# Decode attention over paged latents: pages laid over 32 partitions, values split around the next scores, one maximum per row, and all page loads issued by SP

## The reference

```python
def mla_paged_attn(q_nope, q_rope, ckv, krope, w_uk, w_uv, cache_ckv, cache_krope, page_table):
    past_ckv = cache_ckv[page_table].reshape(B, -1, KV_LORA)      # 8 samples x 4096 tokens x 256
    past_kr = cache_krope[page_table].reshape(B, -1, QK_ROPE)     # ... x 32
    q_lat = jnp.einsum('blhd,chd->blhc', q_nope, w_uk)
    s_past = (jnp.einsum('blhc,btc->bhlt', q_lat, past_ckv)
              + jnp.einsum('blhr,btr->bhlt', q_rope, past_kr)).astype(jnp.float32) * ATTN_SCALE
    s_new = (...) # the same against the sample's own new token
    p = jax.nn.softmax(jnp.concatenate([s_past, s_new], axis=-1), axis=-1)
    o_lat = (jnp.einsum('bhlt,btc->blhc', p[..., :T], past_ckv)
             + jnp.einsum('bhls,bsc->blhc', p[..., T:], ckv))
    return jnp.einsum('blhc,chd->blhd', o_lat, w_uv)
```

## Time and profile before

| | us |
|---|---|
| median of 3 runs (1593.17 to 1598.28) | 1594.5 |
| the profiled execution, its own time | 1593.95 |
| its span in the trace | 1592.3 |
| PE busy | 1354.5 (85%) |
| DVE busy | 979.7 (62%) |
| ACT busy | 638.1 (40%) |
| POOL busy | 220.3 (14%) |

### The profile page before, as it was taken

How to read it: one execution, slowest core, us unless ns; L and a number is a source line. 1 busy time by engine, 2 the same in 40 slices (tenths; PEclk the granted TensorE clock), 3 DMA queues, 4 the chain that set the end, 5 groups by cost and what they waited for, 6 DMA issues and landing times. The chain is left out here.

```text
span 1592.3 us, 26749 instructions
## 1 busy us (share of the span) xinstructions
PE 1354.5 (85%) x9613; PEld 1084.7 (68%) x9613; DVE 979.7 (62%) x1338; ACT 638.1 (40%) x856; POOL 220.3 (14%) x322
## 2 busy tenths in 40 slices
PE   5989999786688877766789982899999999937997
PEld 4989999776344444333568872687888888825886
DVE  5456556663577765454244445788888888845653
ACT  5222434320366611101232100777777777743221
POOL 6000221051100032232000000000000000012210
PEclk9999999898799988878779995899999999977999
DMA  5121111375994055464262221479656999935410
GB/s 185 31 79 41 57 67 54 126 251 155 283 371 113 1 169 161 143 217 152 80 226 106 96 90 66 148 263 363 230 211 235 331 404 405 379 143 214 159 67 40
DMA packets 121049, 275.20 MB, mean 173 GB/s; under 512 B 23601, under 2 KB 44594, under 8 KB 120626
## 3 DMA queue, kind: packets, MB, share of 16 engines
q1 hardware_dynamic: 100578, 200.64, 37.1%
q0 software_dynamic: 17200, 61.63, 10.9%
q10 hardware_dynamic: 3168, 11.54, 1.8%
HBM read 214.34 MB, written 58.38 MB: 171 GB/s over the span
## 5 line engine op out<-in xcount | busy, mean ns | idle before, releaser
L399 PE MATMUL pb<-xH,wH 128*128 128x344 f32 x432 | 143.1, 331 | 25.1 <-DVE wL L858 11.0
L401 PE MATMUL pb<-xH,wL 128*128 128x344 f32 x432 | 140.8, 326 | 0.0
L400 PE MATMUL pb<-xL,wH 128*128 128x344 f32 x432 | 140.8, 326 | 0.0
L1621 DVE STREAM_TRANSPOSE pgT<-pages 128x2304 f32<-128x2304 f32 x32 | 81.8, 2570 | 83.4 <-DMA pages<-in_cache 74.5
L2463 DVE TENSOR_TENSOR downL<-raw_down,downH 128x2048 fp32r<-128x2048 f32 x44 | 98.9, 2288 | 45.2 <-ACT downH L2365 45.2
L1492 PE MATMUL pb<-pgT,q 32*8 32x256 f32 x2304 | 79.1, 432 | 44.6 <-DVE pgT L1621 41.9
L2365 ACT CAST gateH<-raw_gate 128x2048 fp32r<-128x2048 f32 x44 | 83.9, 1911 | 67.5 <-PE pb L2298 41.5
L2463 DVE TENSOR_TENSOR gateL<-raw_gate,gateH 128x2048 fp32r<-128x2048 f32 x44 | 100.5, 2287 | 15.8 <-ACT gateH L2365 15.8
L399 PEld LDWEIGHTS pb<-xH,wH 128*128 128x128 f32 x432 | 83.8, 194 | 27.3 <-issue 10.9
L2463 DVE TENSOR_TENSOR upL<-raw_up,upH 128x2048 fp32r<-128x2048 f32 x44 | 100.3, 2281 | 1.0 <-ACT upH L2365 1.0
L1492 PEld LDWEIGHTS pb<-pgT,q 32*8 32x8 f32 x2304 | 41.5, 94 | 81.8 <-DVE pgT L1621 44.9
(11 more groups left out here) (436 smaller groups left out, 3246.7 us busy)
## 6 DMA issues: line engine op xcount, KB each, us to landing
raw_gate<-in_w_gate SPq DMA_DIRECT2D x32, 1024.0 KB, 7.4
raw_up<-in_w_up SPq DMA_DIRECT2D x32, 1024.0 KB, 7.8
raw_down<-in_w_down SPq DMA_DIRECT2D x32, 1024.0 KB, 8.0
pages<-in_cache SPq DMA_DIRECT2D x144, 144.0 KB, 3.6
y_d<-yzero POOLq DMA_DIRECT2D x4, 4096.0 KB, 31.7
pages<-in_cache POOLq DMA_DIRECT2D x112, 144.0 KB, 3.7
y_d<-yo ACTq DMA_DIRECT2D x22, 512.0 KB, 4.1
wraw_p<-in_w_blk SPq DMA_DIRECT2D x18, 512.0 KB, 3.5
```

The source lines that it names most:

```text
L399: pe.matmul(out, wh, xh, start=first, stop=False)
L400: pe.matmul(out, wh, xl, start=False, stop=False)
L401: return pe.matmul(out, wl, xh, start=False, stop=last)
L1621: dve.transpose(pgT[:, 8 * g:8 * g + 8, :], group_pages(4 * b + g)).then_inc(S("pgT_rdy"), 1)
```

## The change

1. **Pages in 32 partitions.** A page's DMA went to 128 partitions with one token of 1152 bytes in each. Now four tokens that follow one another in memory, 4608 bytes, go to one partition, and a page fills 32 partitions: page n of a group goes to partitions 32(n mod 4) and up. A DMA moves the same 144 KB as 32 runs in place of 128. The group fills the same slot.
2. **All page loads by SP.** POOL issues none. SP looks up 8 page numbers for a group and issues 8 DMAs.
3. **A maximum per row.** The exponents take the negated maximum of their own row (`nmx3`) as bias, and wait for DVE alone. The bound over the four groups of a head is still formed, and from it a weight per row, `part_w`, which scales the sums (`part_s`) and the result (`rden3`).
4. **Values split around the next scores.** PE's list is, for each b: second half of the values of b-1, turned exponents of b, maximum of b, first half of the values of b, bound of b, scores of b+1, sums of b. A half is now four of the eight page places of all four groups. `spv_mm` is raised after each half, and a slot is free after the second.
5. DVE turns one group of the next sample between its small steps, where it turned two together.

The diff, cut to its core:

```diff
-        SHARE = {'sp': (0, 4), 'pool': (4, 4)}
+        SHARE = {"sp": (0, 8)}
...
             for m, page in enumerate(found):
-                eng.dma_start(group_pages(at)[:, first + m, :], cache[bass.ds(page, 1), :, :].rearrange("a p w -> (a p) w")).then_inc(page_sw[at % RING3] if name == "pool" else page_in[at % RING3], 16)
+                n = first + m
+                dst = group_pages(at)[32 * (n % 4):32 * (n % 4) + 32, n // 4 * 4:n // 4 * 4 + 4, :]
+                eng.dma_start(dst, cache[bass.ds(page, 1), :, :].rearrange("a (p s) w -> (a p) s w", s=4)).then_inc(page_in[at % RING3], 16)
...
             if at >= RING3:
-                eng.wait_ge(S("spv_mm"), (at - RING3) // 4 + 1)
+                eng.wait_ge(S("spv_mm"), 2 * ((at - RING3) // 4) + 2)
...
+            def sums(b):
+                pe.wait_ge(S("part_s_rdy"), b + 1)
                 for m in range(2):
-                    pe.matmul(pb[:, 5, H:H + 1], same[:, :, :].rearrange("p c r -> p (c r)"), rs[:, m:m + 1], start=m == 0, stop=m == 1, skip_group_check=True)
-                pe.transpose(pb[0:32, 5, 0:H], pnew[:, :], ident[0:H, 0:H]).then_inc(S("sums_mm"), 1)
+                    last = pe.matmul(pb[:, 5, H:H + 1], same[:, :, :].rearrange("p c r -> p (c r)"), part_s[:, m:m + 1], start=m == 0, stop=m == 1, skip_group_check=True)
+                last.then_inc(S("sums_mm"), 1)
...
                 for x in some:
-                    q = x % 4
-                    last = pe.matmul(pb[32 * q:32 * q + H, 7, 0:KL], pT[b % 2][:, x % 8, x // 8, :], group_pages(4 * b + x // 8)[:, x % 8, 0:KL], start=x < 4,
-                                     stop=x >= PAGES - 4 and q > 0, skip_group_check=True, tile_position=(0, 32 * q))
...
+                    for c in range(4):
+                        last = pe.matmul(pb[32 * c:32 * c + H, 7, 0:KL], pT[b % 2][:, x, c, :], group_pages(4 * b + c)[:, x, 0:KL], start=x == 0,
+                                         stop=x == 7 and c > 0, skip_group_check=True, tile_position=(0, 32 * c))
...
-            for at in range(4, GRPS):
-                load_share(pool, "pool", at)
...
             def exps(b):
+                act.wait_ge(S("nmx3_rdy"), b + 1)
...
+            def part_weights(b):
                 act.wait_ge(S("nb_mm"), b + 1)
...
+                act.activation(part_w[:, :], smx[:, b % 2:b % 2 + 1], ACT.Exp, bias=nb[:, :], scale=SCALE).then_inc(S("part_w_rdy"), 1)
...
+                dve.tensor_scalar(nmx3[:, :], smx[:, at], -SCALE, None, ALU.mult).then_inc(S("nmx3_rdy"), 1)
...
+            def part_sums(b):
+                dve.wait_ge(S("part_w_rdy"), b + 1)
...
+                dve.tensor_scalar(part_s[:, :], rs[:, b % 2, :], part_w[:, :], None, ALU.mult).then_inc(S("part_s_rdy"), 1)
```

More of the change, by code:

```diff
@@ L1256, in load_pages @@
             for m, page in enumerate(found):
-                eng.dma_start(group_pages(at)[:, first + m, :], cache[bass.ds(page, 1), :, :].rearrange("a p w -> (a p) w")).then_inc(page_sw[at % RING3] if name == "pool" else page_in[at % RING3], 16)
+                n = first + m
+                dst = group_pages(at)[32 * (n % 4):32 * (n % 4) + 32, n // 4 * 4:n // 4 * 4 + 4, :]
+                eng.dma_start(dst, cache[bass.ds(page, 1), :, :].rearrange("a (p s) w -> (a p) s w", s=4)).then_inc(page_in[at % RING3], 16)
         def pages_in(eng, at):
[L1261 to L1264, removed]
+            eng.wait_ge(page_in[at % RING3], 128 * (at // RING3) + 128)
         def load_share(eng, name, at):
             if at >= RING3:
-                eng.wait_ge(S("spv_mm"), (at - RING3) // 4 + 1)
+                eng.wait_ge(S("spv_mm"), 2 * ((at - RING3) // 4) + 2)
             load_pages(eng, name, at, *SHARE[name])
@@ L1511, in turn_probs @@
                     pe.wait_ge(S("pT_rdy"), b)
-                    pe.wait_ge(S("rden3_rdy"), b)
+                    pe.wait_ge(S("pTn_rdy"), b)
                 for x in range(8):
-                    last = pe.matmul(pb[:, 4, 32 * x:32 * x + 32], pexp[:, x, :, :].rearrange("p g t -> p (g t)"), heads, start=True, stop=True)
-                last.then_inc(S("pT_tr"), 1)
+                    pe.matmul(pb[:, 4, 32 * x:32 * x + 32], pexp[:, x, :, :].rearrange("p g t -> p (g t)"), heads, start=True, stop=True)
+                pe.transpose(pb[0:32, 4, 256:256 + H], pnew[:, :], ident[0:H, 0:H]).then_inc(S("pT_tr"), 1)
+            def sums(b):
+                pe.wait_ge(S("part_s_rdy"), b + 1)
                 for m in range(2):
-                    pe.matmul(pb[:, 5, H:H + 1], same[:, :, :].rearrange("p c r -> p (c r)"), rs[:, m:m + 1], start=m == 0, stop=m == 1, skip_group_check=True)
-                pe.transpose(pb[0:32, 5, 0:H], pnew[:, :], ident[0:H, 0:H]).then_inc(S("sums_mm"), 1)
+                    last = pe.matmul(pb[:, 5, H:H + 1], same[:, :, :].rearrange("p c r -> p (c r)"), part_s[:, m:m + 1], start=m == 0, stop=m == 1, skip_group_check=True)
+                last.then_inc(S("sums_mm"), 1)
             def weigh(b, some):
@@ L1525, in weigh @@
                 for x in some:
-                    q = x % 4
-                    last = pe.matmul(pb[32 * q:32 * q + H, 7, 0:KL], pT[b % 2][:, x % 8, x // 8, :], group_pages(4 * b + x // 8)[:, x % 8, 0:KL], start=x < 4,
-                                     stop=x >= PAGES - 4 and q > 0, skip_group_check=True, tile_position=(0, 32 * q))
-                if some[-1] == PAGES - 1:
+                    for c in range(4):
+                        last = pe.matmul(pb[32 * c:32 * c + H, 7, 0:KL], pT[b % 2][:, x, c, :], group_pages(4 * b + c)[:, x, 0:KL], start=x == 0,
+                                         stop=x == 7 and c > 0, skip_group_check=True, tile_position=(0, 32 * c))
+                if some[-1] == 7:
                     pe.wait_ge(S("pTn_rdy"), b + 1)
-                    pe.matmul(pb[0:H, 7, 0:KL], pTn[:, :], ckvn[:, :], start=False, stop=True, skip_group_check=True,
-                              tile_position=(0, 0)).then_inc(S("spv_mm"), 1)
+                    last = pe.matmul(pb[0:H, 7, 0:KL], pTn[:, :], ckvn[:, :], start=False, stop=True, skip_group_check=True,
+                                     tile_position=(0, 0))
+                last.then_inc(S("spv_mm"), 1)
             pe.wait_ge(S("q4_rdy"), 2)
@@ L1538, in _ @@
             pe.wait_ge(S("small_zero"), 5)
[L1539 to L1550, removed]
+            for b in range(NB):
+                if b:
+                    weigh(b - 1, range(4, 8))
+                turn_probs(b)
+                largest_row(b)
+                weigh(b, range(0, 4))
+                bound_column(b)
+                if b + 1 < NB:
+                    scores(b + 1)
+                sums(b)
+            weigh(NB - 1, range(4, 8))
             pe.wait_ge(S("o_rdy"), NB)
@@ L1580, in exps @@
             def exps(b):
+                act.wait_ge(S("nmx3_rdy"), b + 1)
+                if b:
+                    act.wait_ge(S("pT_tr"), b)
+                if b >= 2:
+                    act.wait_ge(S("part_s_rdy"), b - 1)
+                n = b % 2
+                act.activation(pexp[:, :, :, :].rearrange("p x g t -> p g x t"), past.rearrange("p g (x t) -> p g x t", x=8), ACT.Exp, bias=nmx3[:, :], scale=SCALE,
+                               accum_out=rs[:, n, 0:1]).then_inc(S("sexp_rdy"), 1)
+                act.activation(pnew[:, :], snew_s[:, :], ACT.Exp, bias=nmx3[0:H, :], scale=SCALE, accum_out=rs[0:H, n, 1:2]).then_inc(S("sexp_rdy"), 1)
+            def part_weights(b):
                 act.wait_ge(S("nb_mm"), b + 1)
                 if b:
-                    act.wait_ge(S("sexp_rdy"), 2 * b)
+                    act.wait_ge(S("part_w_rdy"), b)
                 act.copy(nb[:, :], pb[:, 6, P:P + 1]).then_inc(S("nb_rdy"), 1)
@@ L1586, in exps @@
                 if b:
[L1587 to L1590, removed]
+                    act.wait_ge(S("scale_rdy"), b)
+                act.activation(part_w[:, :], smx[:, b % 2:b % 2 + 1], ACT.Exp, bias=nb[:, :], scale=SCALE).then_inc(S("part_w_rdy"), 1)
             def turned_probs(b):
@@ L1607, in _ @@
             act.wait_ge(S("small_zero"), 5)
[L1608 to L1613, removed]
+            for b in range(NB):
+                exps(b)
+                if b:
+                    latent_out(b - 1)
+                turned_probs(b)
+                part_weights(b)
+            latent_out(NB - 1)
         @block.vector
```

52 lines of the change are left out of this document (33 added, 19 removed).

## The result

The changed kernel took **1611.26 us** (median of 4 runs, 1610.73 to 1611.64) against 1594.05 of the kernel before in the same session (4 runs). The ratio is 1.0096, with a 95% interval from 1.0077 to 1.0115: 17 us slower, where +9 was forecast. The cause runs much as forecast; some terms of its size were off, and the change hides a large gain and a large loss that the forecast's rivals had mis-priced.

A forecast was written before the change was run, and what follows sets the result against it. The prediction took a ring of DVE and SP waiting for each other as the bound, with SP's issuing setting the new pace. Last landing +1.1, stalls +9 and end -0.8 gave +9.3 on 1593.95: 1603 us, range 1580 to 1624.

The forecast's parts named there:

- What bounds the kernel: Kernel before: no engine is full; DVE waits 74.5 us for pages, SP 75.5 us for releases, each for the other.
- SP sets the pace: Changed kernel's page loads: slots free 5 us before SP asks, 26 us a sample; with stalls 1599 to 1612, chance 0.46.
- The ring of the old order: Kernel before: release, lookup, three groups, row maxima and values make one turn, 24 to 28 us a sample.
- A group costs SP 6.5 us: SP's lookup and eight page issues for a group take 6.5 us; twenty-eight groups are 182 us.
- Stalls of 9 us: SP's issues stop now and then, 0.04 us a page over 224 pages: 9 us, between 0 and 18.
- they go away with fewer runs: Rival on SP's stalls: they come from long queues, which 32 runs shorten; +0.3 us, 1594; its range 1590 to 1599, 0.23.
- Last landing 2.2 us after issue: End of SP's page loads: the last page lands 2.2 us after issue, at 756.0 before stalls, against 754.9 now.
- 32 partitions slow the transfer, but inside 6.5 us: Page DMAs: 260 GB/s when full instead of 321, a group 4.5 us, hidden inside SP's 6.5; costs only last landing.
- The end of the stage, 21.0 us: From the last group's turning to the last value: 21.0 us against 21.8 now, 0.8 less.
- The new ring at 20.0 us a sample: New order: a release waits for one group alone, including 8.6 us to landing and 5.1 for half the scores; 20.0 us.
- the rival at 1563: SP does not set the pace: the 20.0 us ring runs six times, 1563 us; fully or in part 1563 to 1589, 0.17.
- Issuing from several engines: Skill rule: sequencer saving usually small; prediction disagreed here, a page taking 0.52 us to issue, 0.46 to 0.57 to move.

The follow-up runs named there:

- e4: Kernel before with one edit, SP alone loads all pages (128 partitions, old order): 1654.2 us, ratio 1.0355.
- e7: Changed kernel with pages over 128 partitions and lookups for groups 0 to 4 only, group 4's numbers reused later: 1552.6 us, ratio 0.9747.
- e3: Changed kernel with pages over 128 partitions again, SP still alone: 1615.1 us, ratio 1.0109.
- e11: Changed kernel, SP alone, with each page on every fourth partition in place of 32 neighbours: 1643.2 us, ratio 1.0306.
- e1: Changed kernel with POOL again loading the last four pages of each group, 32 neighbouring partitions kept: 1590.6 us, ratio 0.9958.
- e2: Changed kernel with pages over 128 partitions and loaded by SP and POOL, leaving new order and row maxima: 1550.7 us, ratio 0.9707.
- e5: Kernel before with the 32-partition layout alone, old order, SP and POOL issuing: 1630.2 us, ratio 1.0230.
- e6: Changed kernel, SP alone, with lookups for groups 0 to 4 only and group 4's numbers reused later: 1571.1 us, ratio 0.9882.
- e10: Changed kernel with SP and POOL issuing, both reusing group 4's page numbers for all later groups: 1598.7 us, ratio 1.0038.
- e9: Changed kernel with SP and POOL issuing and each page on every fourth partition in place of 32 neighbours: 1553.2 us, ratio 0.9732.

## Why the prediction was right, and where its size was off

**What bounds the kernel; SP sets the pace: right.** The ring of the old order is seen in e4, where SP alone still waits for it. For the changed kernel e7 against e3 (instructions taken away, -62 us) and e11 (made dearer, +32) both follow SP's instructions, and SP's wait for releases is 0.7 us. The 1611.3 lies at the upper edge of the 1599 to 1612 that the forecast gave this mechanism.

**A group costs SP 6.5 us: 6.6, by two errors that nearly cancel.** I took 0.23 us off because the table load took 0.53 us in the stage before and 0.30 in this one. I put that down to the stage; it belongs to the number of values. Loads of eight take 0.53 us in this stage too (521/525/533 above), and every load of four in e1 and e2 took 0.30. That is 28 x 0.23 = 6.4 us too little. The other way, an issue of 32 runs takes 316 ns, not 333: 224 x 0.017 = 3.8 us too much. Together +2.6; with 6.6 us a group, 28 groups are 184.8 where I had 182. That 6.5 came so close is luck.

**Stalls of 9 us: 13.** From the first lookup at 571.3 to the last issue at 768.8 are 197.5 us; 184.8 less the last issue's own 0.3 is 184.5. That leaves 13.0 us, 0.058 a page, inside the bounds of 0.02 to 0.08. The rival that they go away with fewer runs does not hold, and e3 speaks against the number of runs as their cause: with four times the runs the same subtraction leaves 11.8 us (from 573.0 to 772.1 are 199.1, less 187.3 for 28 groups of 6.7). They sit for the most part in single instructions: 17 of the 224 DMA instructions took 0.346 to 1.521 us in place of 0.316, 10.0 us more in all. What their cause is stays open.

**Last landing 2.2 us after issue: 3.0.** The last page is issued at 768.8 and its group is turned at 771.9. The sum of these errors, +2.6 or 2.8, +4.0 and +0.8, less 0.8 for a first lookup that came earlier (571.3 for 572.1), is the 6.9 us between the last turn as forecast (765.0) and as measured (771.9).

**32 partitions slow the transfer, but inside 6.5 us: right for this kernel, for the reason given.** 260 GB/s when full was the estimate; by the share of the queue in this stage the changed kernel's pages ran at 260 (33.04 MB in 0.636 x 200 us):

```profile
q1 hardware_dynamic: 10752, 33.04, 63.6%
```

**The end of the stage, 21.0 us: 20.7.** The lower clock in L1559 behind it, +1.5 us, was in no term.

**The new ring at 20.0 us a sample: too slow an estimate.** Given pages fast enough it runs at 16.7 us (e2). Two terms were too long: in e2 the release at 688.0 is followed by the turn of the next group at 695.56, 7.6 us where 8.6 stood, and the second half of the scores then takes 4.1 us where 5.1 stood (in the next turn 7.3 and 3.7). So the gain that SP's pace hides was some 45 us (1595.4 - 1550.7) and not the 31 of the rival at 1563. And that rival joined two things that don't go together: the fast ring and the 32-partition layout. With dense loads the layout costs 36 to 40 us (e5, e1 against e2), which I had priced at nothing because I weighed it only at SP's pace. "SP does not set the pace" with this layout would have been 1571 to 1591, as e6 and e1 show.

**Issuing from several engines.** The Trainium skill's rule ("DMA: Bandwidth & Descriptors", Issuing engines are not separate DMA queues) names the right saving, sequencer time, but its "usually small" does not hold here. The measurement decides: 64 us between e2 and e3. e7 agrees in time with the rest of the rule, that a second engine saves only sequencer time (1552.6 against 1550.7); e10 against e6 does not, where the second engine costs 28 us.

## What to carry to other kernels

When loads are addressed by a table, count the issuing engine's whole instruction stream for each transfer, lookups and all, and compare it with the transfer's own time; here 0.82 us of instructions (6.6 us for eight pages) stood against 0.46 us of transfer (144 KB at 320 GB/s), and taking away the second issuer turned a gain of some 45 us into a loss of 20 (e2 and e3). Price a layout at the densest rate that the kernel could ask for, not at the rate of the bottleneck that hides it, and spread a transfer over all partitions rather than over neighbours, with an eye on what the spreading costs the issuer (e11). When a change has several parts, the best version may be the one with half of them: new order and a maximum per row with the old loads take 1550.7 us (1547.9 with the lookup ahead), 2.9% under the kernel before.

## What the hardware showed unexpectedly

- A DMA to 32 neighbouring partitions costs SP 316 ns to issue, to 128 partitions 333, and to every fourth of 128 partitions 472; for POOL the same three take 489, 539 and 523 ns. The same 32 runs are thus dearer to issue when they are spread, and e9 bears it because two engines share the issues; e11, with one, does not.
- Loading 8 numbers from the table into SP's registers takes 0.52 to 0.53 us, loading 4 takes 0.30.
- Full DMA engines move more with two engines issuing to spread pages (320 GB/s in e2, 322 in e9) than with one (e7: 33.04 MB in 0.767 x 148 us, 291). Into 32 neighbours it makes little difference (e1 240, e6 239, e10 232), and yet two engines issuing are slower there than one. The row is e7's, from 572 to 720 us:

```profile
q1 hardware_dynamic: 32256, 33.04, 76.7%
```
